# The dense part of a hybrid decoder layer: loops replaced by one unrolled order of products

## What is computed

```python
h = rms_norm(x, g_mix)
q, k, v, xb, yb, ga, gb = split(h @ w_in)
a_out = attention(q, k, v) @ w_oa                    # merge width 512
hr = conv_rglru(xb)                                  # below
b_out = (hr * gelu(yb)) @ w_ob
x = x + (sigmoid(ga) * a_out + sigmoid(gb) * b_out) @ w_o
x = x + square(relu(rms_norm(x, g_mlp) @ w_up)) @ w_down          # 4096 wide
x = x + sigmoid(rms_norm(x, g_ple) @ w_ple_gate) * (pe @ w_ple_in)

# conv_rglru: a causal conv of width 4 gives xc, then per channel
r, i = sigmoid(xc @ w_rg_a + b_rg_a), sigmoid(xc @ w_rg_i + b_rg_i)   # 16 diagonal blocks of 64
log_a = 8 * r * log_sigmoid(lam); a = exp(log_a)
h_t = a_t * h_(t-1) + sqrt(-expm1(2 * log_a)) * (i * xc)
```

## Time and profile before

| what | value |
|---|---|
| median of three runs | 2617.09 us (2616.27 to 2618.40) |
| span of the profiled execution | 2609.2 us |
| instructions in it | 35502 |
| TensorE matmuls busy | 2348.6 us, 90% of the span, 13651 of them |
| VectorE busy | 901.2 us, 35% |
| ScalarE busy | 694.0 us, 27% |
| GpSimd busy | 670.5 us, 26% |
| first dense product | 1017.24 us from the start |
| mean granted clock of TensorE | 0.939 of full speed |

### The profile page before, as it was taken

One profiled execution on the slowest core, in us unless ns is written; L12 is line 12 of the kernel. 1 busy time (PEld: TensorE's weight loads), 2 busy tenths in 40 slices (PEclk: granted clock), 3 DMA queues, 4 the chain that ended last, 5 costly groups with the idle time before them and its releaser, 6 DMA issues.

```text
span 2609.2 us, 35502 instructions
## 1 busy us (share of the span) xinstructions
PE 2348.6 (90%) x13651; PEld 2313.3 (89%) x13651; DVE 901.2 (35%) x1601; ACT 694.0 (27%) x1423; POOL 670.5 (26%) x478
## 2 busy tenths in 40 slices
PE   2789998998998954998897999999999999999988
PEld 0789998998998954998887999989999999999988
DVE  6355346346336424006555112322111021121154
ACT  3231232232233212325555223211011011011141
POOL 1131122113013102224432222434233133233241
PEclk7899999899898956999998999999999999999999
DMA  3212222222221222111111112211111111111112
GB/s 109 71 59 100 77 72 92 76 80 68 89 76 43 85 64 78 44 53 46 37 37 32 40 49 66 82 41 49 41 41 49 49 41 49 49 41 49 58 33 83
DMA packets 60500, 156.64 MB, mean 60 GB/s; under 512 B 8596, under 2 KB 29595, under 8 KB 57255
## 3 DMA queue, kind: packets, MB, share of 16 engines
q1 hardware_dynamic: 60360, 154.71, 18.5%
HBM read 140.19 MB, written 16.86 MB: 60 GB/s over the span
## 4 chain that ended last, share of the span: by engine, by line
PE 52%; issue 6%; POOL 2%; ACT 1%; DVE 0%; DMA 0%; POOLq 0%; ACTq 0%; DVEq 0%
PE d_ps L1156 51%; POOL w_lo L1358 1%; POOL xc_lo L1369 1%; PE d_ps L1179 0%; ACT w_hi L1255 0%; POOL g_lo L1366 0%; POOL tmp L1381 0%; PE d_tot L1165 0%; DMA p_raw<-p_t 0%; ACT xcat L1287 0%; ACT L1336 0%; DVE act_lo L1395 0%; DVE x_res L1467 0%; DVE tmp L1505 0%; DVE p_lo L1395 0%
## 5 line engine op out<-in xcount | busy, mean ns | idle before, releaser
L1358 POOL TENSOR_TENSOR w_lo<-w_raw,w_hi 128x1024 fp32r<-128x1024 f32 (+1 forms) x130 | 321.4, 2472 | 715.6 <-ACT w_hi L1255 715.6
L1156 PE MATMUL d_ps<-act_lo,w_hi 128*128 128x352 f32 x1728 | 374.5, 324 | 70.3 <-POOL w_lo L1358 65.1
L880 PE MATMUL at_proj<-qkv_hi,act_lo 128*128 128x384 f32 x864 | 344.7, 399 | 96.5 <-DVE qkv_lo L702 96.5
L1156 PE MATMUL d_ps<-act_hi,w_hi 128*128 128x352 f32 x1728 | 374.4, 325 | 0.0
L1156 PE MATMUL d_ps<-act_hi,w_lo 128*128 128x352 f32 x1728 | 372.8, 324 | 0.0
L1156 PEld LDWEIGHTS d_ps<-act_lo,w_hi 128*128 128x128 f32 x1728 | 297.2, 189 | 72.1 <-issue 64.7
L880 PE MATMUL at_proj<-qkv_hi,act_hi 128*128 128x384 f32 x864 | 331.2, 383 | 0.0
L880 PE MATMUL at_proj<-qkv_lo,act_hi 128*128 128x384 f32 x864 | 330.5, 383 | 0.0
L880 PEld LDWEIGHTS at_proj<-qkv_hi,act_lo 128*128 128x128 f32 x864 | 238.5, 276 | 98.7 <-issue 56.2
L1156 PEld LDWEIGHTS d_ps<-act_hi,w_hi 128*128 128x128 f32 x1728 | 295.4, 189 | 0.0
L1156 PE MATMUL d_ps<-b_lo,w_hi 128*128 128x352 f32 x1248 | 273.0, 327 | 24.2 <-POOL w_lo L1358 18.1
(11 more groups left out here) (213 smaller groups left out, 2609.4 us busy)
## 6 DMA issues: line engine op xcount, KB each, us to landing
w_raw<-w_stream SPq DMA_DIRECT2D x122, 512.0 KB, 3.5
qkv_raw<-w_qkv SPq DMA_DIRECT2D x12, 1536.0 KB, 6.6
vcache<-vc SPq DMA_DIRECT2D x12, 1024.0 KB, 5.0
kcache<-kc SPq DMA_DIRECT2D x16, 512.0 KB, 4.4
e_bc<-lse_dram SPq DMA_DIRECT2D x15, 528.0 KB, 5.3
x_in<-x_t SPq DMA_DIRECT2D x8, 528.0 KB, 7.7
tmp<-x_t SPq DMA_DIRECT2D x8, 528.0 KB, 3.6
y_t<-x_res SPq DMA_DIRECT2D x8, 528.0 KB, 3.9
```

The source lines that it names most:

```text
L880: ins = pe.matmul(pj[i % 3][:, 0:3 * HD], tile_cols(x, k, g, i), w[:, k], start=first, stop=last)
L1156: ins = pe.matmul(ps[s][:, c, 0:CH], w[:, slot, k0 + k], x[:, k, c * CH:(c + 1) * CH], start=k == 0 and x is lo, stop=k == nk - 1 and w is ...
L1358: pool.tensor_tensor(w_lo[:, s, 0:nk], w_raw[:, s, 0:nk], w_hi[:, s, 0:nk].bitcast(F32), ALU.subtract).then_inc(S["wlo"], 1)
```

## The change

All loops of `dense` are unrolled from one list of products, written out on the host; the position of a product in it gives every wait its count. What the arithmetic does stays, except that a sigmoid of the recurrence gates is written as (1 + tanh(x/2))/2. In the new list

- the recurrent branch is first. The two gates of block m-1 are run between xb(m) and yb(m), so conv and split of block m have a block of time. z is split to `b_hi`, `b_lo` block by block; there are two buffers of `xc` and only one of gelu;
- gb and bo follow, gb two ahead, then ga and oa in the same way, with the attention loaded when bo is done; u is split as its blocks end;
- the sums of squares are taken inside the first up product and in the middle of pin; p is loaded and split during the last down products, and the second norm's input is made while they run;
- the last gate product runs chunk by chunk, and its output is stored by chunk;
- on ScalarE and GpSimd the split of the weights stands behind the other work of an up or gt product, no longer ahead of it.

GpSimd's product `ri*xc` goes to VectorE. The scratch tiles of the recurrence lie in the not yet used `X`.

The core of the diff. The order:

```diff
+    for m in range(KD):
+        order.append(("xb", m, 0))
+        if m:
+            order += [("rg", m - 1, 1), ("ig", m - 1, 0)]
+        order.append(("yb", m, 1))
+    order += [("gb", 0, 0), ("rg", KD - 1, 1), ("ig", KD - 1, 0), ("gb", 1, 1)]
+    for m in range(KD):
+        order.append(("bo", m, 0 if m < KD - 1 else 1))
+        if m + 2 < KD:
+            order.append(("gb", m + 2, 1))
+    order += [("ga", 0, 0), ("ga", 1, 1)]
+    for m in range(KD):
+        order.append(("oa", m, 0 if m < KD - 1 else 1))
+        if m + 2 < KD:
+            order.append(("ga", m + 2, 1))
+    order += [("wo", m, m % 2) for m in range(KD)]
+    for kb in range(FB):
+        order += [("up", KD * kb + i, i % 2) for i in range(KD)] + [("down", KD * kb + i, i % 2) for i in range(KD)]
+    order += [("pin", m, m % 2) for m in range(KD)] + [("gt", m, m % 2) for m in range(KD)]
```

SyncE (a unit is one load of weights; units are counted in the list's order):

```diff
-        def load_lru(m, y):
-            for s in range(2):
-                load_w(N0[LRU] + 2 * m + s, s, KD + 2 * m + s)
-            sp.wait_ge(S["mm"], BUMP + T0[LRU])
+        def load_lru(m):
+            y = m % 2
             sp.wait_ge(S["save"], BUMP + m - 1)
             sp.wait_ge(S["z"], BUMP + m - 1)
+            sp.wait_ge(S["rows"], BUMP + m - 1)
             sp.dma_start(prm[:, y], a["lru_prm"][m]).then_inc(S[f"prm{y}_loaded"], 16)
...
+        def load_x(m):
+            sp.wait_ge(S["u"], BUMP + KD)
             if m >= 2:
-                sp.wait_ge(S[f"ev{m % 2}"], BUMP + (T0[WO] + m - 2) // 2 + 1)
+                sp.wait_ge(S[f"ev{m % 2}"], evicted("wo", m - 2))
             sp.dma_start(G[2 + m % 2][:], a["x_t"][:, m]).then_inc(S[f"x{m % 2}_loaded"], 16)
...
+        for u in range(NU):
+            name, m = units[u]
+            load_w(u)
+            if name == "xb":
+                load_lru(m)
+            if name == "yb" and m >= 2:
+                store_state(m - 2)
+            if name == "bo" and m < 2:
+                store_state(KD - 2 + m)
+            if name == "ga" and m == 1:
+                load_att()
+            if name == "wo":
+                load_x(m)
+            if name == "down" and m == KD * (FB - 1) + 2:
+                load_p()
```

ScalarE, from the recurrent branch to wo:

```diff
+        def split(u):
+
+            if u >= NU:
+                return
+            s, n = u % 2, depth(u)
+            if u >= 2:
+                act.wait_ge(S["mm"], mm_of(*last_of[u - 2]))
+            act.wait_ge(S[f"w{s}_loaded"], BUMP + 16 * (u // 2 + 1))
+            act.activation(w_hi[:, s, 0:n], w_raw[:, s, 0:n], ACT.Copy).then_inc(S["whi"], 1)
...
+        def gelu(m):
+            act.wait_ge(S["z"], BUMP + m)
+            act.wait_ge(S["mm"], mm_of("yb", m))
+            act.activation(c3(G[2][:]), out3(1), ACT.Gelu_apprx_tanh).then_inc(S["ev1"], 1)
...
+        for m in range(1, KD):
+            evict_xb(m)
+            rows(m)
+            split(unit[("xb", m)] + 2)
+            gate_tanh(m - 1)
+            gate_weights(m)
+            decay(m - 1)
+            conv_hi(m)
+            root(m - 1)
+            split(unit[("yb", m)] + 2)
+            z_part(m - 1)
+            gelu(m)
...
         for m in range(KD):
-            product(m % 2, N0[WO] + m, m % 2, act_hi, act_lo, (T0[WO] + m) // 2, ready=("u_lo", 0))
...
+            split(unit[("oa", m)] + 2)
+            if m + 2 < KD:
+                gate_a(m + 2)
+                split(unit[("ga", m + 2)] + 2)
+            if m == KD - 3:
+                for k in range(m):
+                    u_part(k)
+            if m >= KD - 3:
+                u_part(m)
```

More of the change, by code:

```diff
@@ L1026, in dense @@
[L1026 to L1033, removed]
+    prm = in_last("lru_prm", [P, 2, 39])
+    hb = in_last("half_bias", [P, 2, 2])
+    tmp8 = in_last("tmp8", [P, DB])
@@ L1040, in dense @@
         S[n] = sem("d_" + n)
-    for n in ("whi wlo mm ev0 ev1 att_hi att_lo init "
-              "ghi glo cv rows xc_hi xc_lo la ex_a th den rec qd root_b ix bd h0m h0a h0z scan z save "
+    for n in ("whi wlo mm ev0 ev1 att_hi att_lo init half "
+              "ghi glo cv rows xc_hi xc_lo la ex_a th den qd root_b ix bd h0m h0a h0z scan z save "
               "z_hi z_lo u u_hi u_lo "
@@ L1112, in _, with load_att @@
[L1112 to L1120, removed]
+        def load_att():
+            sp.wait_ge(S["mm"], mm_of("bo", KD - 1))
+            for j in range(HG):
+                sp.dma_start(att_raw[:, j], att_dram[j + 1]).then_inc(S["att_loaded"], 16)
@@ L1129, in _, with load_p @@
[L1129 to L1136, removed]
+        def load_p():
+            sp.wait_ge(S["hid_lo"], BUMP + FB * KD)
+            for k in range(PKD):
+                sp.dma_start(p_raw[k][:], a["p_t"][:, k]).then_inc(S[f"p{k}_loaded"], 16)
@@ L1165, in column_sums @@
                 pe.matmul(tot[:, c % 2, 0:CH], ones[:], G[1][:, c * CH:(c + 1) * CH], start=True, stop=True).then_inc(S["tot"], 1)
[L1167 to L1181, removed]
@@ new lines, in _ @@
+        for key in ((name, m) for name, m, s in order):
+            name, m = key
+            if name in ("xb", "yb", "gb", "ga"):
+                product(key, act_hi, act_lo)
+            elif name == "rg":
+                gate(key, 0)
+            elif name == "ig":
+                gate(key, 1)
+            elif name == "bo":
+                product(key, b_hi, b_lo, ready=("z_lo", 0))
+            elif name == "oa":
+                product(key, b_hi, b_lo, nk=HG, ready=("att_lo", 0))
+            elif name == "wo":
+                product(key, act_hi, act_lo, ready=("u_lo", 0))
+            elif name == "up":
+                product(key, b_hi, b_lo, ready=("b_lo", 0), inside=5 if m == 0 else None)
+            elif name == "down":
+                product(key, act_hi, act_lo, ready=("hid_lo", KD * (m // KD)))
+            elif name == "pin":
+                if m == KD // 2:
+                    column_sums(1)
+                product(key, p_hi, p_lo, nk=PKD, k0=PKD * (m % 4), ready=("p_lo", 0))
+            elif m < KD - 1:
+                product(key, b_hi, b_lo, ready=("b_lo", KD))
+            else:
+                product_by_chunk(key, b_hi, b_lo, ready=("b_lo", KD))
@@ new lines, in _ @@
+                roots(1)
+            act.wait_ge(S["mm"], mm_of("pin", m))
+            act.activation(c3(pe_out[:, m]), out3(m % 2), ACT.Copy).then_inc(S[f"ev{m % 2}"], 1)
+            if m % 4 == 3:
+                split(unit[("pin", m)] + 2)
+        for m in (KD - 2, KD - 1):
+            scaled_hi(m, 1)
+        for m in range(KD - 1):
+            act.wait_ge(S[f"ev{m % 2}"], evicted("gt", m))
+            act.activation(G[2 * (m % 2)][:], G[2 * (m % 2)][:], ACT.Sigmoid).then_inc(S["sg"], 1)
+            split(unit[("gt", m)] + 2)
@@ L1387, in _, with split, gate_weights @@
-        walk(pool, split, step)
+        def split(u):
+            if u >= NU:
+                return
+            s, n = u % 2, depth(u)
+            pool.wait_ge(S["whi"], BUMP + u + 1)
+            pool.tensor_tensor(w_lo[:, s, 0:n], w_raw[:, s, 0:n], w_hi[:, s, 0:n].bitcast(F32), ALU.subtract).then_inc(S["wlo"], 1)
+        def gate_weights(m):
+            pool.wait_ge(S["ghi"], BUMP + m + 1)
+            pool.tensor_tensor(g_lo[:], g_raw[:], g_hi[:].bitcast(F32), ALU.subtract).then_inc(S["glo"], 1)
@@ new lines, in _ @@
+        pool.memset(xcat[:, 0:3], 0.0).then_inc(S["init"], 1)
+        split(0)
+        split(1)
+        split(2)
+        gate_weights(0)
+        conv_lo(0)
+        split(3)
+        for m in range(1, KD):
+            split(unit[("xb", m)] + 2)
+            gate_weights(m)
+            conv_lo(m)
+            split(unit[("yb", m)] + 2)
+        for u in range(unit[("gb", 0)] + 2, unit[("wo", 0)] + 2):
+            split(u)
+        for m in range(KD):
+            split(unit[("wo", m)] + 2)
+            sum_squares(m, 0)
@@ new lines, in _ @@
+        for i in range(KD * FB):
+            if i == 0:
+                split(unit[("up", 0)] + 2)
+            pool.wait_ge(S["hid_hi"], BUMP + i + 1)
+            pool.tensor_tensor(act_lo[:, i % KD], G[2 * (i % 2)][:], act_hi[:, i % KD].bitcast(F32), ALU.subtract).then_inc(S["hid_lo"], 1)
+            if i:
+                split(unit[("up", i)] + 2)
+            if i % KD == KD - 1:
+                for d in range(i - KD + 1, i + 1):
+                    split(unit[("down", d)] + 2)
+                    m = d - KD * (FB - 1)
+                    if m >= 2:
+                        for k in ([0, 1, 2] if m == 2 else [m]):
+                            sum_squares(k, 1)
@@ L1509, in _, with inverses @@
-        walk(dve, lambda x, s, after, nk=KD: None, step)
+        def inverses(r):
+            for c in range(NCH):
+                dve.wait_ge(S["root"], BUMP + NCH * r + c + 1)
+                part = G[3][:, c * CH:(c + 1) * CH]
+                dve.reciprocal(part, part).then_inc(S["rstd"], 1)
+            dve.wait_ge(S["rstd"], BUMP + NCH * (r + 1))
+        dve.tensor_scalar(clam_h[:], clam[:], 0.5, None, ALU.mult).then_inc(S["half"], 1)
```

(25 more changed lines are left out.)

713 lines of the change are left out of this document (368 added, 345 removed).

## The result

| | before | after |
|---|---|---|
| median of the runs on one chip | 2616.68 us (4 runs, 2609.0 to 2618.4) | 2558.84 us (4 runs, 2556.33 to 2560.36) |
| ratio of the times | | 0.9779, 95% interval 0.9761 to 0.9798 |
| profiled execution: span | 2609.2 us | 2556.4 us (its own time 2558.24) |
| first dense product starts | 1017.24 us | 1014.63 us |
| last product ends | 2601.13 us | 2550.64 us |

The forecast was 2578.3 us with a range from 2563 to 2598.

A forecast was written before the change was run, and what follows sets the result against it. TensorE, busy 90% of the span, was taken as the bound, with only idle time to recover: idle and slow time 53.1 against 89.6 us and an end 2.3 us shorter give 2617.1 - 36.5 - 2.3 = 2578.3 us, range 2563 to 2598.

The forecast's parts named there:

- six waits of gates: Recurrent blocks: TensorE idles before rg while yb's weights queue behind the save on SyncE, 32.4 us in six blocks.
- the stage of wo: Inside wo(0): load_x(0) waits for all u ahead of wo(1)'s weights; stall 6.5 us plus 1.7 for the clock, 8.2 us.
- ga and oa without a stall: Stage of ga and oa: gate and split take 4.6 us under a product of 5.8, cover 1.2 us, nothing on the path.
- the first (queue without effect): Recurrent blocks: the queue doesn't hold them, a block takes 26.2 + 0.8 us, 28 us less, 2551 us; chance 0.08.
- the second (2.4 us more in each block): Recurrent blocks: GpSimd's split and `g_lo` delay VectorE once more, 2.4 us in each of six blocks, 2593 us; chance 0.13.
- the third (straight code): Whole dense part: straight code starves TensorE; loses from 0.1662 us a matmul, at 0.168 ends at 2634 us; chance 0.07.
- the fourth: ScalarE's table switches: a further fixed wait of 1.4 us behind each, 2.1 x 6, 2591 us; chance 0.02.
- the 7.9 us: Whole kernel: the median lies 7.9 us above the profiled span of 2609.2 us, a difference carried into the forecast.
- chain of a held block: Recurrent branch: ScalarE's eviction of xb to the next one, through save, load, split and gelu, takes 31.6 us.
- the first norm's sums: Column sums inside up(0): the third waits 1.3 us for ScalarE's first root with a table load; both norms together 6.2 us.
- for such things: Loops and p: 1.0 us left for cases like ScalarE's split behind an up product's square, 8.7 us under 11.7.
- done by 15.5: Chain of a recurrent block: table load and Sqrt end by 15.5 us, while `xc_lo` holds VectorE's product until about 16.1.

The follow-up runs named there:

- yb_first: Changed kernel with SyncE issuing the weights of yb(m) ahead of the wait for the states of block m-2; 2543.06 us, ratio 0.9714 to before.
- wo1_first: Changed kernel with SyncE issuing the weights of wo(1) ahead of the first load of x; 2554.40 us, ratio 0.9761 to before.
- before_unrolled: Kernel before with the loops of its dense part unrolled and nothing else; 2611.09 us, ratio 0.9984 to before.
- after_again: The changed kernel run once more, unaltered; 2561.62 us, ratio 0.9784 to before, dense part 1536.9 us.
- after_root_first: Changed kernel with ScalarE taking the root of block m-1 ahead of the copy to xc_hi of block m; 2563.78 us in one run, dense part 1543.5 us.
- after_sigmoid: Changed kernel with Sigmoid in place of Tanh in the two recurrence gates; 2559.94 us in one run, dense part 1540.2 us.
- both_first: Changed kernel with SyncE issuing the weights of yb(m) ahead of load_lru(m) and those of wo(1) ahead of load_x(0); 2536.32 us, ratio 0.9693 to before.

## Why the forecast was right, and where it missed

**Right: what takes the place of the removed waits.** That the branch would be held by SyncE's queue, at the weights of yb(2) to yb(7), with the release by gelu, and that load_x(0) would hold wo(0), was read from the diff and from the earlier trace rows, and is shown by yb_first and wo1_first. The single terms: six waits of gates, as told; the stage of wo 8.3 us longer than its matmuls at 0.162, forecast 8.2; the end of the kernel 2.3 us shorter, forecast 2.3; ga and oa without a stall, as told; the pace 0.162. Of the rivals, the first (queue without effect) is refuted by yb_first, the second (2.4 us more in each block) by the 30.6 us, the third (straight code) by before_unrolled, the fourth by the row of gelu 1.30 us behind its load's start.

**Wrong: the size.** The step that failed is the first one below, the 7.9 us carried from the span to the median. With the 1.8 us that the runs show in its place the same working gives 2572.2 us, and its range, moved by as much, holds the measured time. The whole miss, 2578.3 - 2558.8 = 19.5 us, comes from three steps.

1. *"7.9 us above it and I carry that difference."* The step took the distance between one profiled execution and a median as a constant. It is 1.8 us of constant, and the rest was the luck of that execution; in the profile after, time and median are 0.6 us apart, so span and median 2.4. 7.9 - 2.4 = 5.5 us of the miss.
2. *The first product at 1017.24.* It came at 1014.63, and between 1012.2 and 1023.6 in the profiles of this study, with the same code ahead of it. 2.6 us, and their sign is luck. Together with step 1 this is scatter ahead of the dense part, some 8 us, which the range didn't contain: its bounds came from the dense part's costs alone.
3. *The dense part, 1547.4 against 1536.0.* The chain of a held block was 31.6 for 30.6 us (its own terms add up to 31.5): the states were saved 21.5 us behind the copy of xb instead of 21.9, the weights of yb issued 0.9 us behind the save instead of 1.4, and from the split to the end of gelu 4.4 us passed instead of 4.5. That is 6 us in six blocks; the forecast had itself called this its least sure term. Behind the last held block the slow clock didn't come in this execution (1.6; in after_again it came). From up(0) to the end it was 3.7 less: the first norm's sums didn't wait for a table load, which had run ahead of its wait (1.5), and the 1.0 us "for such things" wasn't needed. The pace, a shade under 0.162 us, gives most of what is left.

5.5 + 2.6 + 11.4 = 19.5 us. What holds the blocks is not touched by any of it. Nearly all terms were taken on the same side, which a range made of bounds on single terms doesn't show; and without steps 1 and 2, which are scatter, the forecast would have been 11 us too high and inside its range.

**Right for a reason that was incomplete.** In the chain of a block I let `xc_lo` hold VectorE and the root be "done by 15.5". Both were so (the root ended at 15.7, the product with it started at 16.1), but after_root_first shows that `xc_lo` stands in the better of two places there: moving it saves 1.1 us at this product and costs 2.2 us behind it.

## What to carry to other kernels

When an order is rewritten, look through the queue that issues the loads as through an engine: a wait for a late result, put between two loads, is a wait for everything behind it, and here two such lines were worth 26 us of 2560. Where two engines exclude each other, don't ask whether an operation collides but what runs beside the collision; it is paid only if nothing else was being waited for. And the difference between a profiled execution and the median is mostly scatter (only 1.8 us of it were constant here): forecast on the profile's own time and put the scatter of the runs into the range.

## What the runs showed of the hardware

A two-input operation of VectorE on 8 columns took 0.16 us alone and 2.3 to 2.46 beside GpSimd's `xc_lo` (2.6 to 2.8 us); a scan took 4.38 instead of 2.36 us beside a split of 2.4. GpSimd loses as well: 3.3 us for a split beside the conv, 2.36 where VectorE waits. I had expected the first and not that a long scan is held for what is left of GpSimd's operation.

In the changed kernel TensorE stood still for 2.4 to 3.6 us in front of the gates of six blocks. Behind the first five its clock fell to the lower of its two levels, 1.2 instead of 2.4 GHz: some ten matmuls start 0.29 instead of 0.16 us apart, and the granted clock from 1206.4 to 1209.8 us is 0.50. Behind the sixth, a stop of 2.75 us, it stayed at the upper one. A stop of 3.5 us in wo1_first brought no slow matmul and one of 3.4 some nineteen; in after_sigmoid stops of 2.0 us brought eleven; in both_first those of 0.8 to 1.5 us brought none. So the length of the stop alone doesn't say whether the clock falls, and no run here shows what does. The granted clock in the stretch of the recurrent branch was 0.95 in the changed kernel.

```profile
1014.00:1240.00 226.00, 207.66 (x1212) 205.39 (x1213) 146.28 (x146) 109.53 (x143) 73.31 (x31) 0.95 0.13 43
```
